# A ring of five gather slots in place of six in a hybrid decoder step

## What is computed

```
z = x @ w_in                                  # q, k, v, u, each 512 wide
a = differential attention(q, k, v)           # 4 heads, ALiBi, causal; samples also read a paged cache
s = S5 state space model(u), then a GLU
x = LayerNorm(ALPHA * x + concat(a, s) @ w_out)
x = LayerNorm(ALPHA * x + PEER(x))
```

```
u = u_tab[idx];  v = v_tab[idx]               # rows of 1024 floats
act = gelu(u . x)
out = sum over the 128 experts of (g * act) * v
```

## Time and profile before

| | |
|---|---|
| median of three runs | 3720.8 us |
| the profiled execution | 3718.95 us |
| its span, first to last instruction | 3717.1 us |
| first gather | 391.56 us |
| PE / DVE / ACT / POOL busy | 71% / 65% / 41% / 35% |
| mean granted TensorE clock | 0.786 |
| gathers | 1088, 1 MB each |
| those of prompt tile 2 issued | 1184.6 to 1554.1 us |
| moved by all DMA queues | 1316.27 MB |

### The profile page before, as it was taken

How to read it: one execution, slowest core, us unless ns; L and a number is a source line. 1 busy time by engine, 2 the same in 40 slices (tenths; PEclk the granted TensorE clock), 3 DMA queues, 4 the chain that set the end, 5 groups by cost and what they waited for, 6 DMA issues and landing times.

```text
span 3717.1 us, 44267 instructions
## 1 busy us (share of the span) xinstructions
PE 2644.5 (71%) x14060; PEld 1115.0 (30%) x14060; DVE 2434.5 (65%) x5648; ACT 1511.0 (41%) x4363; POOL 1284.6 (35%) x1099
## 2 busy tenths in 40 slices
PE   7887678876667667766776677667766776777666
PEld 4565445332123212311232123212322232332211
DVE  8703755478557855785678567866786678445875
ACT  1102334344444444434444444444444444544433
POOL 0000233333443344335433443344334433223334
PEclk9968799877787777877787787677877776888866
DMA  5332789999999999999999999999999999998988
GB/s 141 82 116 103 303 310 375 383 401 375 418 374 409 371 416 360 409 371 410 376 406 371 406 371 406 360 414 369 411 378 414 363 399 384 391 392 357 393 335 343
DMA packets 241576, 1316.27 MB, mean 354 GB/s; under 512 B 41682, under 2 KB 69106, under 8 KB 91058
## 3 DMA queue, kind: packets, MB, share of 16 engines
q0 software_dynamic: 156672, 1140.92, 76.3%
q1 hardware_dynamic: 78784, 163.78, 12.6%
q10 hardware_dynamic: 5890, 8.75, 0.7%
HBM read 1293.78 MB, written 17.97 MB: 353 GB/s over the span
## 4 chain that ended last, share of the span: by engine, by line
DVE 31%; DMA 29%; PE 23%; issue 7%; ACT 7%; POOL 2%; SPq 1%; DVEq 0%; POOLq 0%; ACTq 0%
DMA UV<-in_peer_uv,zone_x 26%; DVE zone_z L1518 12%; PE psum L1176 9%; PE psum L1098 4%; PE psum L472 2%; DVE zone_x L1420 2%; DVE zone_x L1423 2%; DVE zone_x L1421 2%; PE psum L337 2%; POOL UV L991 2%; DMA wq<-in_cache_k 2%; DVE zone_x L1422 1%; ACT D L1286 1%; DVE zone_y L1474 1%; DVE zone_z L1482 1%
## 5 line engine op out<-in xcount | busy, mean ns | idle before, releaser
L1176 PE MATMUL psum<-UV,D 64*64 64x512 f32 x8704 | 1521.7, 792 | 934.7 <-ACT D L1286 909.2
L991 POOL DMA_INDIRECT UV<-in_peer_uv,zone_x x1088 | 1279.2, 1176 | 2329.0 <-PE psum L1176 1860.7
L1518 DVE CUSTOM_DVE_ANT_0 zone_z<-UV,zone_x 128x1024 bf16<-128x1024 f32 x1088 | 1333.6, 1226 | 787.1 <-DMA UV<-in_peer_uv,zone_x 722.1
L1281 ACT ACTIVATE ge<-acts 128x1 f32<-128x1 f32 x1088 | 219.7, 202 | 1666.8 <-DVE acts L1518 1662.9
L1176 PEld LDWEIGHTS psum<-UV,D 64*64 64x64 f32 x8704 | 314.6, 160 | 1817.5 <-issue 1785.6
L1286 ACT ACTIVATE D<-id,wge 128x64 f32<-128x64 f32 x1088 | 378.3, 348 | 35.4
L1283 ACT ACTIVATE wge<-ge,zone_x 128x1 f32<-128x1 f32 x1088 | 320.6, 295 | 35.4
L1118 PE MATMUL psum<-wq,zone_z 128*128 128x256 f32 (+1 forms) x1152 | 316.8, 436 | 1.2 <-ACT zone_z L1227 1.2
L1118 PEld LDWEIGHTS psum<-wq,zone_z 128*128 128x128 f32 (+1 forms) x1152 | 242.8, 216 | 122.9 <-issue 71.9
L1281 ACT ACT_TABLE_LOAD x113 | 145.0, 1283 | 2.8 <-ACT vrows L584 0.8
L1098 PE MATMUL psum<-w_out_sb,zone_z 128*128 128x512 f32 (+1 forms) x256 | 115.9, 606 | 0.7 <-DMA w_out_sb<-in_w_out 0.7
(11 more groups left out here) (280 smaller groups left out, 2244.9 us busy)
## 6 DMA issues: line engine op xcount, KB each, us to landing
wq<-in_peer_w_q SPq DMA_DIRECT2D x72, 1024.0 KB, 9.3
UV<-in_peer_uv,zone_x POOLq DMA_INDIRECT x1088
wq<-in_cache_k SPq DMA_DIRECT2D x64, 256.0 KB, 10.1
vrows<-in_cache_v SPq DMA_DIRECT2D x64, 256.0 KB
wq<-in_w_in SPq DMA_DIRECT2D x10, 1024.0 KB, 7.0
zone_x<-in_x_all SPq DMA_DIRECT2D x9, 512.0 KB, 8.2
UV<-in_w_out SPq DMA_DIRECT2D x1, 4096.0 KB, 22.0
w_out_sb<-in_w_out SPq DMA_DIRECT2D x1, 4096.0 KB, 33.3
```

Source lines behind the costliest of these rows:

```text
L991: pool.indirect_dma_start(out=UV[:, n % RING, :], out_offset=None, in_=table, in_offset=bass.IndirectOffsetOnAxis(ap=icur[:, t % 2, column ...
L1176: ins = pe.matmul(bank[6 + r][q:q + 64, :], D[64 * r:64 * r + 64, n % RING, :], UV[64 * r:64 * r + 64, n % RING, DM + 512 * e:DM + 512 * e ...
L1281: act.activation(ge[:, j:j + 1], acts[:, j:j + 1], ACT.Gelu).then_inc(sem("gelu_done"), 1)
L1518: dve.tensor_tensor_reduce(out=junk[:, :], in0=UV[:, n % RING, 0:DM], in1=x1[:, t % 2, :], scale=1.0, scalar=0.0, op0=ALU.mult, op1=ALU.ad ...
```

## The change

RING becomes 5. The tile UV has five slots of 2048 floats per partition instead of six, and D, acts, ge and wge have five entries. The third slot of w_in, which was the ring's last, becomes a tensor of its own, w_in2, of the same 8 KB per partition. Slots 0 to 4, in which the other startup data lie, keep their places in UV. The number of landing semaphores falls to five.

```
-RING = 6
+RING = 5
...
         UV = sb("UV", [P, RING, 2 * DM])
         D = sb("D", [P, RING, SR])
+        w_in2 = sb("w_in2", [P, KC, 256])
         wq = sb("wq", [P, 2, KC, 2 * NKEY])
...
         def w_slot(i):
 
-            slot = wq[:, i % 3, :, :] if i % 3 < 2 else UV[:, RING - 1, :].rearrange("p (k n) -> p k n", k=KC)
+            slot = wq[:, i % 3, :, :] if i % 3 < 2 else w_in2[:, :, :]
             return slot, f"w_in{i % 3}", 16 * (i // 3 + 1)
```

## The result

The changed kernel takes 3908.3 us (median of four runs, 3905.17 to 3912.23) against 3721.6 before: a ratio of 1.050, with a 95% interval of 1.0482 to 1.0518. Slower was forecast, at 3840; the 187 us lost are more than half as much again as the 118 of the sum, and lie in the upper part of the range. The profiled execution took 3912.23 us.

What follows compares the result with a forecast made beforehand. Paced by turns: by the gathers and by what holds up the experts' work on DVE, ACT and PE. 3718.95 us plus 113 for eight prompt tiles and 5 for the sample tile gave 3837, said as 3840; range 3775 to 3920.

Steps and rivals of the forecast that it cites:

- four kinds of stall: Per prompt tile: four softmaxes 6.6 us; output projection, end of last head and start of tile 2.5 each; sum 14.1.
- a slower transfer in a shorter queue: Taken as nothing; 0.1 us for each of 553 waited-for landings, 55 us, kept for the upper end only.
- The slot isn't freed: Rival: the ring gives up 8 KB per partition and the new tensor takes 8 KB; no time changes; no chance given.
- part 2: Moving the third w_in slot to its own tensor: 0 us; ring's first fill also 0, bound one transfer, 2.5 us.
- Softmax: Four per tile: table loads and exponentials on ACT delay slot release; 0.8 to 2.5 us each, middle 1.65, 6.6 per tile.
- the projection: Output projection's matmuls stand ahead of experts on PE, once per tile; queues run dry; a whole transfer, 2.5 us.
- The queues: DMA queues carrying the gathers: full in a calm stretch at 2.5 us per gather; a stall's loss per slot capped at that.
- The slack of about 2 us in a calm stretch: Lateness a release may have before queues run dry: from about 4.5 us to about 2; five slots still feed the queues.
- Hidden anyway: Rival, 8%: the queues make the delays good; 0 to 56 us, 3721 to 3777.
- The 358 GB/s as a limit: Skill page's HBM limit for one core: 3677 us for 1316 MB, memory already the floor, loss about 0.
- Every interruption counts: Rival, 11%: four softmaxes and eight key heads per tile each cost a full transfer; 240 us, 3960.
- Faster, by the clock: Rival, 3%: a PE that pauses more might be granted more clock; at 1.00 instead of 0.77, 197 us less, 3642.

Runs made afterwards that it cites:

- the run with the modulus alone: Ring modulus 5 with memory and weight slot left as in the kernel before: 3904.7 us, ratio 1.0509 to the kernel before.
- the half gathers: Each gather brings 4 KB per row instead of 8, matmuls read the same half, v half left out: 3374.2 us with six slots, 3513.9 with five.
- gathers alone: All other work left out, one to five gathers in flight, then twenty bursts of three into empty queues: 2.49 us per gather with four or five in flight.
- the tanh pair: Experts' gelu replaced by tanh, so the table loads around each exp fall away: 3706.5 us with six slots, 3862.1 with five.
- The release at the dot: Five slots, each free once its dot is done, matmuls reading a fixed tile instead: 3663.8 us, ratio 0.9864 to the kernel before.

## Why the prediction was right, and where it was too small

**Direction, place and carrier** were right. The dots' wait for landings grew by nearly the whole loss, calm stretches hardly changed (419 GB/s against 423), the bytes stayed, and nearly all of the loss lies in the parts with the four kinds of stall that I had named. That the start of a tile lost 2.4 us where I said 2.5 owes something to luck: I had picked a whole transfer between the bounds of nothing and a transfer. **The range** held by luck as well. Its upper bound for the stalls was 145 us, and they cost more. 187 lies inside only because of the 55 us that I had set aside for something else, a slower transfer in a shorter queue. "The slot isn't freed" and part 2's 0 us hold by the run with the modulus alone.

**Softmax, "I take the middle, 1.65"**, is the term that was mis-sized: 12.1 us per tile in tiles 1 to 6 and not 6.6. Over all eight prompt tiles it is 90 us in place of 53, 37 more; the projection's 45 in place of 20 adds 25. These two are 62 of the 75 us between the 118 of the sum and the 193.3 by which the span grew; the other parts add 9 and the sample tile 4. The step that failed is the bound under it: "the most that one slot can lose here, its transfer: 2.5 us". The softmax shown breaks it with 2.7 us, and the half gathers do so more plainly: with transfers of 1.25 us the four softmaxes still lose 8.8 us per tile, 2.2 each, and the projection 4.4. Two things were missing in the walk. The gather behind a late one comes late as well (1.57 us at the softmax shown, about 1 in the bursts of gathers alone). And I took the slack from issues of the six-slot trace, 5.2 us, though with five slots the stretch ahead has already lost one gather of it (7.4 us from issue to landing in place of 10.3).

**"The queues"** as what is lost were the wrong picture for most of it. They were full in the calm stretches and paced them, so that each gather short seemed to be worth a transfer. Halving the transfer took away only a quarter of the loss; taking ACT and PE out of the round took off more time than the loss had been. The sum priced each hole by a transfer; what ran short was the time that a slot has for its whole round, of which the 6 us behind the dot's start don't give way.

**The slack of about 2 us in a calm stretch** was right; three in flight cost 0.06 us each more than four. The term I had left at 0 with an upper bound of 0.1 us per landing is of this kind. By an estimate from these rates it holds at most some 30 us (0.06 x 553); no run separates it.

**Rivals.** "Hidden anyway" is out: 187 us against at most 56. The 358 GB/s as a limit are out as well, for gathers alone ran at 422 GB/s over 120 us. In the Trainium skill's page "DMA: Bandwidth & Descriptors", section "Bandwidth", that figure is also given as the share of a core when both cores of a pair are streaming, and this kernel runs on one core. "Every interruption counts" is out by its place: the experts 108 to 128 and 0 to 20, where the key heads lie, lose 3.1 us per tile together, not eight transfers. By its size it was nearer than my sum (240 us and 118 against 187). "Faster, by the clock" is out: the mean granted clock fell from 0.786 to 0.768, and PE's expert matmuls took 1561 us busy in place of 1522.

**What stays open.** How the 47 us by which the step fell with half the transfer divide into refill, the shorter queue and the transfer proper; and why the tanh pair, with stalls 2.56 us shorter, still loses 10.3 us at the softmaxes. The release at the dot was run with five slots alone, so what a sixth is worth beside it wasn't tried: that an earlier release makes the time shorter is shown, that it makes the step smaller is argued.

## What to carry to other kernels

Judge the depth of a ring by the round of a slot: mean pace times slots, set against the sum of its parts and of the stalls that fall into it. Here the pace was set by full queues in places and 18.2 us of round looked ample over parts of 10.6, and still the sixth slot was worth 5%. Split the round into its parts, and look for those that a missing slot can't squeeze: here the 6 us between dot and next issue, of 18.2. To find what kind of time a slot covers, halve the transfer and see how much of the step from n to n - 1 slots is left, then shorten the hold. Here half the transfer took some 350 us off the kernel of six slots and 390 off that of five and left three quarters of the step, while an earlier release took more off the changed kernel than the slot had cost. A split of the ring that doubles the issues seems to pay only while the issuing engine has room.

## What was new about the hardware

A gather of 1 MB into empty queues is read 5.5 us after its issue. The shortest way from issue to landing was 5.4 us for it and 3.9 for one of half the size (kernel before, half gathers with six slots), so by an estimate from these two some 2.4 us of it don't depend on the size. With one gather in flight one is read every 6.0 us, with two 3.05, with three 2.55, with four 2.49. The second of a burst is read 3.6 us behind the first in the burst shown (3.5 in the median of twenty) though it was issued 1.24 us after it, and only the third is back at 2.5.
